# Three of the weight rests of each second mixer made on GpSimd instead of VectorE

## The reference

```
for l in range(DEPTH):
    h = swiglu_ffn(rmsnorm(x, ffn1_pre_g[l]), ffn1_w_gu[l], ffn1_w_down[l])
    x = x + 0.5 * rmsnorm(h, ffn1_post_g[l])
    h = mixing_sublayer(rmsnorm(x, mix_pre_g[l]), w_in[l], ...)
    x = x + rmsnorm(h, mix_post_g[l])
    h = swiglu_ffn(rmsnorm(x, ffn2_pre_g[l]), ffn2_w_gu[l], ffn2_w_down[l])
    x = x + 0.5 * rmsnorm(h, ffn2_post_g[l])
```

## Time and profile before

| | |
|---|---|
| median of 3 runs | 2960.8 us (2957.74 to 2963.33) |
| the profiled execution, its own time | 2955.16 us |
| span of that execution (first to last instruction) | 2953.4 us |
| mean granted TensorE clock | 0.986 |
| the convolution of the first mixer | about 1972 to 2012 us of the span |
| the convolution of the second mixer | about 2585 to 2625 us |

### The profile page before, as it was taken

The page is one execution under the profiler, slowest core; times in us unless marked ns, Lnnn a source line. Parts: engine busy times, 40 slices in busy tenths (PEclk is TensorE's granted clock), DMA queues, the critical chain, the costliest instruction groups (busy, mean ns, idle before and its releaser), DMA issues.

```text
span 2953.4 us, 34430 instructions
## 1 busy us (share of the span) xinstructions
PE 2833.4 (96%) x13288; PEld 2340.7 (79%) x13288; DVE 2061.2 (70%) x2999; ACT 1706.6 (58%) x2373; POOL 32.6 (1%) x55
## 2 busy tenths in 40 slices
PE   7999999999998999999999989999899999888999
PEld 5888888788876888888888868777778788776787
DVE  5577655657767989888988955587665554787554
ACT  5555554555565777777777754455454544554543
POOL 0000000000001000000000000000000000000000
PEclk9999999999998999999999999999999999999999
DMA  6444455453356999999999955554455555444453
GB/s 217 157 134 135 160 194 186 161 171 129 129 194 225 362 354 356 347 346 359 351 344 352 358 179 185 179 171 143 145 187 183 190 185 187 163 151 148 164 185 114
DMA packets 173979, 633.65 MB, mean 215 GB/s; under 512 B 19584, under 2 KB 19584, under 8 KB 173808
## 3 DMA queue, kind: packets, MB, share of 16 engines
q1 hardware_dynamic: 171072, 621.88, 60.9%
q0 software_dynamic: 2736, 9.49, 0.9%
HBM read 629.20 MB, written 2.10 MB: 214 GB/s over the span
## 4 chain that ended last, share of the span: by engine, by line
PE 86%; DVE 8%; ACT 3%; issue 1%; DMA 1%; SPq 0%; DVEq 0%; ACTq 0%
PE ps L1485 26%; PE ps L1487 26%; PE ps L1486 26%; DVE wlo L823 3%; PE ps L1655 2%; DVE CA L1349 2%; PE ps L1739 1%; PE ps L1790 1%; ACT whi L326 1%; DVE XL L853 1%; DMA raw<-in_W 1%; ACT XH L348 1%; PE ps L1641 1%; PE ps L1642 1%; PE ps L1542 0%
## 5 line engine op out<-in xcount | busy, mean ns | idle before, releaser
L823 DVE TENSOR_TENSOR wlo<-raw,whi 128x1024 fp32r<-128x1024 f32 x1182 | 1386.0, 1221 | 453.5 <-ACT whi L326 447.0
L326 ACT ACTIVATE whi<-raw 128x1024 fp32r<-128x1024 f32 x1182 | 1187.9, 1058 | 495.9 <-PE ps L1487 488.1
L1485 PE MATMUL ps<-whi,XH 128*128 128x512 f32 (+1 forms) x2064 | 821.6, 398 | 52.6 <-DVE XL L853 39.7
L1487 PE MATMUL ps<-whi,XL 128*128 128x512 f32 (+1 forms) x2064 | 806.8, 391 | 0.0
L1486 PE MATMUL ps<-wlo,XH 128*128 128x512 f32 (+1 forms) x2064 | 806.8, 391 | 0.0
L1485 PEld LDWEIGHTS ps<-whi,XH 128*128 128x128 f32 x2064 | 392.3, 190 | 141.9 <-issue 24.6
L1487 PEld LDWEIGHTS ps<-whi,XL 128*128 128x128 f32 x2064 | 391.9, 190 | 82.4
L1486 PEld LDWEIGHTS ps<-wlo,XH 128*128 128x128 f32 x2064 | 392.7, 190 | 76.8 <-issue 0.5
L1485 PE MATMUL ps<-whi,XEH 128*128 128x512 f32 x704 | 280.9, 399 | 3.1 <-DVE wlo L823 1.7
L1487 PE MATMUL ps<-whi,XEL 128*128 128x512 f32 x704 | 275.2, 391 | 0.0
L1486 PE MATMUL ps<-wlo,XEH 128*128 128x512 f32 x704 | 274.1, 389 | 0.0
(11 more groups left out here) (365 smaller groups left out, 2648.4 us busy)
## 6 DMA issues: line engine op xcount, KB each, us to landing
raw<-in_W SPq DMA_DIRECT2D x1182, 512.0 KB, 4.9
GP<-in_ffn_post_g POOLq DMA_DIRECT2D x4, 512.0 KB, 4.0
X<-in_x SPq DMA_DIRECT2D x4, 256.0 KB, 3.9
skew<-RB POOLq DMA_DIRECT2D x4, 256.0 KB, 6.0
RB<-skew POOLq DMA_DIRECT2D x8, 128.0 KB, 6.6
GP<-in_mix_post_g POOLq DMA_DIRECT2D x2, 512.0 KB, 3.8
out<-X SPq DMA_DIRECT2D x2, 512.0 KB, 2.6
mload<-in_cum_sums POOLq DMA_DIRECT2D x1, 768.0 KB, 9.3
```

The source lines that it names most:

```text
L326: act.activation(k.whi[:, slot, part], k.raw[:, at, part], ACT.Copy).then_inc(*k.up("act_hi"))
L823: dve.tensor_tensor(k.wlo[:, at, part], k.raw[:, at, part], k.whi[:, slot, part], ALU.subtract).then_inc(*k.up("dve_lo"))
L1485: pe.matmul(ps, xh, k.whi[:, slot, cols], start=first, stop=False)
L1487: return pe.matmul(ps, xl, k.whi[:, slot, cols], start=False, stop=last)
```

## The change

In each second mixer three slabs, those of offset 11, 13 and 15, are marked as pooled. VectorE's `lo` skips a marked slab: it counts it, and issues nothing. GpSimd gets a `lo` of its own, which does the same two subtractions of 128x1024 for a given slab and raises a new semaphore, `pool_lo`. It makes the three rests one after the other, behind the second masking of the scores and ahead of the load of the next gain. Its halves wait for `act_hi` as VectorE's did. TensorE waits before each slab on the counter that belongs to it, with the counts corrected for the skipped ones. The slabs' places in `raw` and `whi`, the order on TensorE and ScalarE, and all arithmetic stay.

```diff
+MIX2_BASE = [MOE_BASE + NE * FF_SLABS + FF_SLABS + l * (2 * FF_SLABS + MIX2_SLABS) for l in range(2)]
+POOL_RESTS = [[MIX2_BASE[l] + i for i in (11, 13, 15)] for l in range(2)]
...
+    def pooled(self, n):
+
+        return self.shift == 0 and n in POOL_RESTS[0] + POOL_RESTS[1]
...
             if self.n == self.limit:
                 return
+            if self.pooled(self.n):
+                self.n += 1
+                continue
             slot, at = self.slot(), self.place_of()
...
-        pe.wait_ge(k.of("dve_lo"), 2 * self.n + 2)
+        self.rests(self.n)
...
+    def rests(self, n):
+
+        pe, k = self.eng, self.k
+        pooled = sum(self.pooled(m) for m in range(n + 1))
+        if self.pooled(n):
+            pe.wait_ge(k.of("pool_lo"), 2 * pooled)
+        else:
+            pe.wait_ge(k.of("dve_lo"), 2 * (n + 1 - pooled))
...
-                    pe.wait_ge(k.of("dve_lo"), 2 * (self.n - 2 + s) + 2)
+                    self.rests(self.n - 2 + s)
...
+    def lo(self, n):
+
+        pool, k = self.eng, self.k
+        for h in range(2):
+            part = slice(h * HALF, (h + 1) * HALF)
+            pool.wait_ge(k.of("act_hi"), 2 * n + h + 1)
+            pool.tensor_tensor(k.wlo[:, n % RAW, part], k.raw[:, n % RAW, part], k.whi[:, n % RING, part], ALU.subtract).then_inc(*k.up("pool_lo"))
...
         self.causal(T + "n0", T + "n1", 0)
+        for n in POOL_RESTS[l]:
+            self.lo(n)
         self.post_gain(f"g2{l}p", [T + "p.out11"], "ffn2_post_g_2", l)
```

## The result

The change makes the kernel slower: 2970.07 us median of 7 runs (2963.78 to 2972.62) against 2960.61 us of 7 runs of the kernel before, ratio 1.0033, 95% interval 1.0022 to 1.0045, that is 6.5 to 13.3 us. The forecast was 2975 us, in a range of 2957 to 2986, +14.8 us, slower with a chance of 0.75.

The account below looks back on a forecast made before the run. It took VectorE's unbroken chain from tap 0 to tap 30 to price the convolution, with TensorE waiting on it. 2 x (13.2 - 6.8 + 1.0) = +14.8 us on the 2960.8 median gave a forecast of 2975 us, range 2957 to 2986.

Parts of the forecast that it names:

- The mechanism: In the convolution, each GpSimd instruction is inserted into VectorE's chain, as taps and rests read two SBUF operands.
- three observations beside selects: Old trace: two selects and VectorE rests delayed each other (0.20, 0.24 us lost); four PSUM-reading VectorE instructions were not slowed.
- term 1: Three rests per mixer leave VectorE's chain ahead of tap 30, saving 3 x 2.27 = 6.81 us per mixer.
- The hold: Time each GpSimd instruction keeps VectorE's convolution waiting: 2.2 us, six per mixer, adding 13.2 us per mixer.
- bounds by the slope (1.87): Hold estimate from select times: 0.91 ns per element times 2048 elements read, 1.87 us without the fixed part.
- the scaled row (2.53): Hold estimate from the 0.63 us select of 128x512, doubled for length and again for inputs: 2.53 us.
- The bound of 1.6 us: Lower hold estimate: 0.20 us lost by VectorE per 256 elements GpSimd reads, so 1.6 us for 2048.
- The clock: TensorE's longer waits bring more half-rate clock around the convolution's end: 1 us per mixer, range 0 to 3.4.
- The replay: First mixer's convolution: TensorE waits 2 to 5 us for slab 12, about 7 for slab 14; tap 30 ends near 2018.
- Parallel work: Rival: GpSimd's tensor_tensor runs beside the convolution's taps without exclusion; gain 13.3 us, time 2947; chance 0.12.
- break-even: Rival: hold of 0.9 to 1.6 us in the convolution, kernel within 0.2%, 2958 to 2966 us; chance 0.13.
- GpSimd as a new bound: Rival: hold past 2.5 us or GpSimd waiting between halves makes its rests late for TensorE, 2981 to 2995 us; chance 0.15.

Follow-up runs that it names:

- d_two: Kernel before plus six GpSimd tensor_tensor of 128x896 per second mixer, one SBUF tile as both operands, result unread: 2972.06 us, ratio 1.0048.
- d_none: Kernel before plus six GpSimd zero fills of 128x896 per second mixer, reading nothing: 2961.62 us, ratio 1.0004.
- e_topk: The change with slabs 7 and 8 pooled, during the search, instead of 11, 13, 15, and VectorE's later rests spread anew: 2943.5 us, ratio 0.9938 to kernel before.
- d_one: Kernel before plus six GpSimd copies of 128x896 per second mixer, one SBUF operand, result unread: 2971.04 us, ratio 1.0040.

## Why the prediction was right

**The mechanism** was the one forecast. The three observations beside selects in the kernel before carried over to `tensor_tensor`: `d_two` shows the insertion with no consumer, `d_none` that only reads of GpSimd matter, `e_topk` that it depends on what VectorE reads. The Trainium skill (SBUF — State Buffer, Who interferes with whom) has a VectorE instruction with two SBUF inputs contend with a GpSimd instruction that reads SBUF and not with one that only writes it; `d_two` (1.4 us per hold) and `d_none` (none) agree. By the same section a VectorE instruction with at most one SBUF input does not contend, unless it runs in a mode that uses both of VectorE's ports; the search in `e_topk` agrees, and the mask at 0.95 us in place of 0.43 may be the exception, though no run here shows its mode. The section has the second one blocked for the whole of the first instruction; here the hold was 2.09 of 2.40 us.

**The removed rests** saved what term 1 said, 3 x 2.27 us: six holds of 2.09 us less 6.8 make 5.7 us per mixer, and the convolutions got 5.8 and 5.7 us longer.

**The hold** was set at 2.2 us and measured 2.09. Alone the instruction takes 2.40 us, and 0.3 us of that does not hold VectorE. The prediction used 2.2 us for both, so two errors, an instruction taken as too short and a hold taken as the whole of it, cancelled in part. That, and the choice of the middle between two bounds, was luck in part. The bounds by the slope (1.87) and by the scaled row (2.53) enclose it. `d_one` shows why doubling by the number of operands falls short: a copy holds 0.62 us for 896 elements, two different tiles 1.82, so two operands cost nearly three times one. The bound of 1.6 us rested on a proportionality that does not hold.

**The clock** is the term that was mis-sized. It was put at +1 us per mixer; the profiled execution gives about +0.7 us in the first; in the second `channel_sum` starts 0.9 us behind the tap, but the half-rate stretch that cost 1.7 us behind the last tap before now lies ahead of it. Together that is about nothing in place of 2 us. The half-rate stretches beside the longer waits all fell ahead of the last tap, where most of what they cost TensorE only shortened its next wait. With the measured hold, the sum without the clock is 12 x 2.09 - 13.6 = +11.5 us, inside the measured 6.5 to 13.3.

**The replay** was right about which slabs TensorE would wait for, and off on sizes: in the first mixer slab 12 for 5.4 us (2 to 5 forecast), slab 14 for 4.7 (7 forecast), so the longest wait is for slab 12 and not for slab 14, in both mixers. A likely reason, not tested, is that the longer wait for slab 12 delays slab 14's turn. That TensorE would reach the last tap late, by 0.7 us, it missed.

**The rivals.** Parallel work (0.12) and break-even (0.13, a hold of 0.9 to 1.6 us) fall with the 2.09 us hold. GpSimd as a new bound (0.15) does not show: none of TensorE's waits above is for a rest of GpSimd, all four are for rests of VectorE.

## What to carry to other kernels

In this kernel, work on GpSimd that reads SBUF was free beside the search, whose instructions read one tensor. Beside two-operand instructions of VectorE it is inserted into VectorE's queue at GpSimd's slower pace, here 2.09 us for a job that VectorE does in 1.14. Before handing a job over, list what VectorE reads in that stretch: here the search for the best 64 lies some 17 us earlier in the same program (GpSimd's first rest at 1955.48 there, 1972.87 in the change) and hid two rests per mixer, except for 0.5 us at one mask. Look at the durations afterwards too, as that mask reads one operand only. And what is freed must be closed up at once: without moving the rests behind it, most of it turned into a wait for ScalarE.

## What the runs showed of the hardware

A `tensor_tensor` of 128x1024 on GpSimd takes 2.40 us on two different tiles and keeps VectorE's two-operand instructions waiting for 2.09. With one tile as both operands, 128x896, it is 1.68 us at least, against 2.13 with two. I had expected the time to follow the number of elements read and not which tiles they are in. A GpSimd fill of 0.85 us costs VectorE's taps nothing. A `tensor_scalar` of 128x512 on VectorE with one SBUF operand took 0.95 us in place of 0.43 beside GpSimd's `tensor_tensor` (one case), while MAX8 and MATCH_REPLACE8 of 128x256 kept their time.
